# Taking the gathered rows earlier and storing the gates by group

## The reference, cut to what matters

```
u   = take(u_tab, expert)                 # 128 rows of 2048 for each token
act = gelu(einsum('cd,chkd->chk', x, u))
wgt = gate * act
v   = take(v_tab, expert)
y   = einsum('chk,chkd->cd', wgt, v)      # then layer norm of ALPHA * h + y
```

## Time and profile before

| what | value |
|---|---|
| median of 3 runs | 4105.11 us |
| lowest and highest | 4092.33 and 4108.23 us |
| the profiled execution | 4092.33 us |
| its span | 4090.4 us |
| granted PE clock, mean | 0.974 |
| PE, DVE, ACT, POOL busy | 94%, 67%, 34%, 29% of the span |
| moved by DMA | 1240.23 MB, 303 GB/s over the span |

### The profile page before, as it was taken

One profiled execution on the slowest core, in us unless ns is written; L12 is line 12 of the kernel. 1 busy time (PEld: TensorE's weight loads), 2 busy tenths in 40 slices (PEclk: granted clock), 3 DMA queues, 4 the chain that ended last, 5 costly groups with the idle time before them and its releaser, 6 DMA issues.

```text
span 4090.4 us, 61953 instructions
## 1 busy us (share of the span) xinstructions
PE 3847.7 (94%) x24631; PEld 3529.6 (86%) x24631; DVE 2760.7 (67%) x3403; ACT 1394.6 (34%) x1975; POOL 1181.8 (29%) x595
## 2 busy tenths in 40 slices
PE   7899999999888999999999899999998879999997
PEld 7789999999877788888888799999998867777776
DVE  3444455554675555666555478888887879989889
ACT  4444444443313300000000244466663323433332
POOL 0000000000533344444444262212113334435542
PEclk9899999999999999999999899999999999999998
DMA  4235554455367699999999447999999999999996
GB/s 166 83 107 182 185 184 179 182 184 185 135 260 286 248 402 396 391 406 395 403 397 404 191 160 288 378 366 366 369 364 408 411 400 406 411 400 406 382 399 264
DMA packets 209831, 1240.23 MB, mean 303 GB/s; under 512 B 20176, under 2 KB 53024, under 8 KB 65824
## 3 DMA queue, kind: packets, MB, share of 16 engines
q1 hardware_dynamic: 125024, 663.85, 42.5%
q0 software_dynamic: 73728, 536.90, 32.2%
q10 hardware_dynamic: 10944, 37.75, 2.3%
HBM read 1200.68 MB, written 37.75 MB: 303 GB/s over the span
## 4 chain that ended last, share of the span: by engine, by line
PE 76%; DMA 10%; DVE 8%; ACT 3%; issue 2%; SPq 0%; ACTq 0%; POOL 0%; DVEq 0%
PE dense_ps L850 22%; PE dense_ps L839 12%; PE dense_ps L841 12%; PE dense_ps L840 12%; DMA wbuf<-in_peer_v_dram 5%; PE dense_ps L1046 5%; PE dense_ps L878 3%; DVE h L1084 3%; DMA row<-in_peer_v_dram,expert 2%; PE score_ps L1046 2%; DVE w_lo L1134 2%; PE o_ps L939 1%; PE score_ps L1007 1%; DMA wbuf<-in_w_units_dram 1%; PE o_ps L1046 1%
## 5 line engine op out<-in xcount | busy, mean ns | idle before, releaser
L1134 DVE TENSOR_TENSOR w_lo<-wbuf,w_hi_r 128x1024 fp32r<-128x1024 f32 x804 | 977.9, 1224 | 557.1 <-ACT w_hi_r L528 556.7
L528 ACT ACTIVATE w_hi_r<-wbuf 128x1024 fp32r<-128x1024 f32 x876 | 919.3, 1058 | 1243.7 <-PE dense_ps L841 678.8
L839 PE MATMUL dense_ps<-act_hi,w_hi_r 128*128 128x256 f32 x4160 | 1196.8, 288 | 35.2 <-DVE w_lo L1134 31.5
L840 PE MATMUL dense_ps<-act_lo,w_hi_r 128*128 128x256 f32 x4160 | 1185.6, 285 | 0.0
L841 PE MATMUL dense_ps<-act_hi,w_lo 128*128 128x256 f32 x4160 | 1185.3, 285 | 0.0
L839 PEld LDWEIGHTS dense_ps<-act_hi,w_hi_r 128*128 128x128 f32 x4160 | 806.9, 194 | 47.5 <-DVE w_lo L1134 33.6
L840 PEld LDWEIGHTS dense_ps<-act_lo,w_hi_r 128*128 128x128 f32 x4160 | 807.0, 194 | 0.0
L841 PEld LDWEIGHTS dense_ps<-act_hi,w_lo 128*128 128x128 f32 x4160 | 806.2, 194 | 0.0
L481 POOL DMA_INDIRECT row<-in_peer_v_dram,expert x256 | 529.6, 2069 | 954.8 <-DVE h L1084 925.0
L850 PE MATMUL dense_ps<-xT,wbuf 128*128 128x256 f32 x3200 | 705.4, 381 | 0.7 <-ACT xT L513 0.7
L481 POOL DMA_INDIRECT row<-in_peer_u_dram,expert x256 | 476.7, 1862 | 743.7 <-DVE row L1079 642.2
(11 more groups left out here) (199 smaller groups left out, 4293.0 us busy)
## 6 DMA issues: line engine op xcount, KB each, us to landing
wbuf<-in_w_units_dram SPq DMA_DIRECT2D x460, 1024.0 KB, 5.9
wbuf<-in_peer_v_dram SPq DMA_DIRECT2D x128, 1024.0 KB, 11.3
act_spill<-stage ACTq DMA_DIRECT2D x64, 256.0 KB, 8.1
gate_spill<-gbuf ACTq DMA_DIRECT2D x8, 2048.0 KB, 10.7
e_act<-act_spill SPq DMA_DIRECT2D x32, 512.0 KB, 12.2
e_gate<-gate_spill SPq DMA_DIRECT2D x32, 512.0 KB, 14.1
cT<-in_x_dram SPq DMA_DIRECT2D x2, 2048.0 KB, 10.0
row<-in_peer_u_dram,expert POOLq DMA_INDIRECT x256, 12.2
```

Of the source, the lines that this page charges most:

```text
L528: act.activation(w_hi[:, j, :], wbuf[n % 2][:, j, :], ACT.Copy).then_inc(w_hi_ready, 1)
L839: nc.tensor.matmul(out, w[0], x[0], start=opens, stop=False)
L840: nc.tensor.matmul(out, w[0], x[1], start=False, stop=False)
L1134: V.tensor_tensor(w_lo[n % 2][:, j, :], wbuf[n % 2][:, j, :], w_hi[:, j, :].bitcast(F32), ALU.subtract).then_inc(lo_by_dve, 1)
```

## The change

Three edits. `rows_in` for the units of the V stage gives 3 rows in each odd unit and 2 in each even one; it gave 3 in every tenth unit, 2 in the others, and none from the 62nd on. The statistics of the second tile move from unit 62 to unit 61. And `gate_spill` is laid out by chunk, group, partition and 128 numbers, where it was by chunk, partition, group: the store of a chunk then writes for each partition 32 pieces of 512 bytes, 64 KB apart, where it wrote one piece of 16 KB; the load of a group reads for each chunk one stretch of 64 KB, where it read 128 pieces of 512 bytes, 16 KB apart. On the SBUF side nothing changes.

```diff
-STATS_AT, SD_AT, APPLY_AT, OUT_AT = (19, 62), (21, 62), (24, 63), (27, 63)
+STATS_AT, SD_AT, APPLY_AT, OUT_AT = (19, 61), (21, 62), (24, 63), (27, 63)
...
     if m >= 0:
-        return 0 if m > 61 else 3 if m % 10 == 0 else 2
+        return 3 if m % 2 else 2
...
-        gate_spill = nc.dram_tensor("gate_spill", (HALF // GCHUNK, P, GROUPS, 4 * GCHUNK), F32, kind="Internal").ap()
+        gate_spill = nc.dram_tensor("gate_spill", (HALF // GCHUNK, GROUPS, P, 4 * GCHUNK), F32, kind="Internal").ap()
...
-                gates = gate_spill[:, :, bass.ds(2 * i + q, 1), :].rearrange("c p o x -> p c (o x)")
+                gates = gate_spill[:, q, :, :] if q < 2 else \
+                    gate_spill[:, bass.ds(2 * i + q, 1), :, :].rearrange("c o p x -> c (o p) x")
...
                 sp.dma_start(e_gate[q % 2][:, :, :, :].rearrange("p c b t -> p c (b t)"),
-                             gates).then_inc(e_in[q % 2], 16)
+                             gates.rearrange("c p x -> p c x")).then_inc(e_in[q % 2], 16)
...
-                act.dma_start(gate_spill[ck, :, :, :].rearrange("p q x -> p (q x)"),
-                              gbuf[ck % 2][:, :, :].rearrange("p k t -> p (k t)")).then_inc(gate_sent, 16)
+                act.dma_start(gate_spill[ck, :, :, :].rearrange("q p x -> p q x"),
+                              gbuf[ck % 2][:, :, :].rearrange("p (q b) t -> p q (b t)", b=4)).then_inc(gate_sent, 16)
```

## The result

The changed kernel is slower: 4201.26 us (median of 4 runs, 4194.47 to 4208.65) against 4106.67 us (4 runs, 4092.33 to 4110.24), a ratio of 1.0238 with a 95% interval of 1.0205 to 1.0270. The prediction was 4197 us. The profiled execution took 4196.56 us with a span of 4194.8 us, 104.4 us over that of before.

The account below looks back on a forecast made before the run. The prediction took PE to bound the U stage's middle and DMA the V stage. Profiled 4092.3 us + 40.6 (V stage and tail) + 51 (U stage) = 4184, or 4197 us as median; range 4130 to 4285.

Parts of the forecast that it names:

- V stage bound by DMA: V stage: DMA engines' throughput, not PE or DVE, sets the pace until near its end; share 1.01 in 50 units.
- 20 more gathers in the first 50 units, +51.4 us: V stage, first 50 units: 20 more row gathers at 2.57 us each lengthen them from 623.6 to 675.0 us.
- The last 14 units, -6.9 us: V stage's end: no gathers left, so units run at PE's pace, 152.3 us in place of 159.2.
- Tail -3.9 us: After the V stage: statistics in unit 61 leave DVE free 7.2 us into the last unit, gaining 3.9 us.
- Gate read, no gain: V stage's gate loads: pieces stay 512 bytes, so no gain; as a bound 0.7 us a read, 23 us in all.
- The hold on ACT: U stage: each gate write holds ACT's next DMA 9.6 us; PE loses 6 us in each of seven, 42 us.
- The cover: U stage: PE can absorb 4.6 us of a late act block before it has to wait.
- The eighth write, +9 us: U stage: ACT waits for the last gate write to its end, 9 us longer; bounds +1 and +26.
- (1): U stage: gate write isn't felt, V stage's 40.6 us stand alone; 4148 us in the median's terms; chance 0.20.
- (2): U stage: gate write much worse, 120 us or more; 4265 us in the median's terms; chance 0.14.
- (3): V stage: compact gate reads free it to run at PE's pace; 4065 us in the median's terms; chance 0.04.
- (4): V stage: earlier rows cost nothing and the write isn't felt; 4094 us in the median's terms; chance 0.07.

Follow-up runs that it names:

- e10: e1 with DVE taking only half of each gathered row in the V stage, gathers whole; 4133.78 us in one run, first 50 V units 667.2 us.
- e5: Kernel before with gates laid out by group, partition, chunk: writes in 512-byte pieces, reads in 4 KB runs; 4141.99 us, ratio 1.0090.
- e2: Kernel before with only the change's new gate_spill layout, its write and read; rows and statistics as before; 4169.35 us, ratio 1.0148.
- e4_spread: Kernel before with the new gate layout, each write cut into quarters sent in separate units, ACT's wait four units later; 4116.14 us, ratio 1.0032.
- e1: Kernel before with only the change's row rule and earlier statistics, gates stored as before; 4144.71 us, ratio 1.0083.
- e3_pairs: Kernel before with gates laid out by chunk, pair of groups, partition, written in 1 KB pieces; rows as before; 4109.36 us, ratio 1.0015.

## Why the prediction was right, point by point

**V stage bound by DMA: right.** The share stayed at 1.01 and the stretch grew. e10 (DVE's work taken away) and e5 (DMA time taken away) show it from both sides. A unit took 13.2 us until unit 49, where I had 13.5. **20 more gathers in the first 50 units, +51.4 us: somewhat too high.** The DMA view of the first 50 units, of the kernel before and then of the changed one (q0 has the gathers: packets, MB, share of the engines):

```profile
DMA packets 60885, 249.89 MB, mean 401 GB/s; under 512 B 4225, under 2 KB 30321, under 8 KB 33649
...
q0 software_dynamic: 15698, 114.31, 44.9%
```

```profile
DMA packets 62470, 267.93 MB, mean 405 GB/s; under 512 B 4493, under 2 KB 29647, under 8 KB 32971
...
q0 software_dynamic: 18334, 133.56, 49.1%
```

133.56 - 114.31 = 19.25 MB, or 18.4 rows of 1.0486 MB, and the engines moved 405 GB/s in place of 401. 18.04 MB more in all at 405 GB/s are 44.5 us; the better rate gives back 6.2 us of the 623.6: +38.3, and +38.2 was measured. So of the 13.2 us that 51.4 was too high, some 4 are the 1.6 rows fewer, 3 the other queues' traffic, and 6 the room in the rate, for which the bounds allowed 9. **The last 14 units, -6.9 us: wrong.** They gave +0.8. I had all gathers out by unit 49, from DVE's sections; but DVE's section of a unit splits the weights of the one two ahead, and when it ends PE is about two units further by its own count. By PE's count the last gather was issued in unit 51:

```profile
4034.70 5.08 POOL L482 DMA_INDIRECT row<-in_peer_v_dram,expert  x1 [1.72 <-DVE h L1085]
```

So units 50 to 53 were still bound by DMA. The windows of units 50 to 54 and 55 to 62:

```profile
4011.30:4073.30 62.00, 56.57 (x241) 44.49 (x240) 53.12 (x37) 23.52 (x23) 13.12 (x6) 1.00 0.89 341
4073.30:4160.40 87.10, 87.10 (x386) 72.09 (x385) 46.25 (x39) 36.85 (x35) 0.00 (x0) 1.00 0.57 205
```

The later eight ran at PE's pace, 10.9 us each, as forecast for all 14; the five before them took 12.4 us each, 7.6 us too many in all, which is what the term lacked. The two errors lie in one place and partly cancel: +44.5 was predicted for the stage, +39.0 measured.

**Tail -3.9 us:** -2.7. The statistics of unit 61 ran only at 4160.09, ahead of the last split, and DVE was free 8.3 us into the unit, not 7.2.

**Gate read, no gain: about right.** The V stage in e2 and the change lie 5.1 and 5.7 us under the matching kernels with the old layout (777.7 against 782.8; 821.8 against 827.5), but e4_spread, with the same compact reads as e2, has 785.4, so a gain isn't shown.

**The hold on ACT: right in mechanism, too small.** Predicted 9.6 us at 50% of the engines with release at 72 pieces left; the profile has 11.1 to 13.9 us for six of seven writes (one 3.6), at a mean of 43%, and in the one shown with release at some 33. The single share of 50% was the wrong picture: the write ran first almost alone and then at 13.8%. The 24% of the upper bound, for both other queues at work, comes from no row, and was still too high for that part. The cover came out right: the issue took 13.4 in place of 0.3 us and PE waited 8.1, so 5.0 us were covered in the one shown, 4.6 predicted. The stretch grew by 53.5 us, 42 predicted as seven losses of 6. Measured were six waits of 7.4 and none at the seventh write, 41.8 us more waiting than before, so that this near hit is in part luck; what the sum had at nothing is the clock behind each wait (11.7 us more of busy time). **The eighth write, +9 us:** ACT waited 9.7 us longer. Units 48 to 63 grew by 18, of which up to 8 lie in the scatter of that stretch.

In sum: U stage +71.5 where I had +51, V stage and tail +36.3 where I had +40.6, in one execution; ahead of unit 16 it is 3.4 us shorter, for no known reason. So the profiled execution grew by 104.4 us and I had 91.6; the medians moved by 94.6 us. The forecast went from the profiled execution of before, which lies 12.8 us under its median, while that of after lies 4.7 under its own. That the median came within 4 us of the forecast is therefore partly luck, and it owes something to errors of opposite signs.

The rivals: (1) the unfelt write fell with e2's profile, (2) the much heavier one with the U stage's +71.5 us, where it wanted 120 (the two rival queues were not always busy), (3) the freed V stage with e2's 777.7 us and e5's 759.3, (4) with e1. The Trainium skill's 512 bytes for line rate ("DMA: Bandwidth & Descriptors", Specifications) is not borne out: e5's stretch with its reads in 4 KB runs moved 414 GB/s where the kernel before, with the same reads in pieces of 512 bytes, moved 401.

Open: why the gathers reached the engines later behind the sixth write, though GpSimd issued one 2.5 us after it as after the third; and whether the eighth write's longer wait is all of units 48 to 63's growth, since the stretch scatters.

## What to carry to other kernels

Count a store's pieces on each DMA engine, not only its bytes: in this kernel a queue that had its fill held the next DMA on it, and with that every copy that ACT owed to PE (13.4 us behind 256 pieces an engine). Cut such a store into parts with gaps behind them, or give it longer runs. Where a stage is bound by DMA, transfers moved earlier within it only leave the engines empty at its end; move them out of it.

## What the runs showed of the hardware that I had not expected

When the held issues of the changed kernel ended, 3,285 to 3,568 of the 4,096 pieces had begun, so 33 to 51 an engine were left on average. With pieces of 1 KB (e3_pairs) an issue that took 0.53 us ended with 83 an engine left of 128, one of 1.25 us with 72, and the one of 3.87 us with 24. I had estimated one limit of 72 from SP's rows; one number doesn't describe these, and what sets the release stays open.

PE's granted clock was 0.50 when it came back from waits of 5.8 to 8.6 us, and 1.00 only 3 to 6 us later; in the six waits of units 16 to 47 this added about 12 us of busy time to 44.5 us of waiting.

A write in 512-byte pieces ran at 25 ns a piece and engine while it was almost alone (2,854 pieces in 4.5 us, 341 GB/s), and had 13.8% of the engines once two queues with mostly 8 KB pieces worked beside it (47.3% and 40.5%).
